# Inverting the delta rule's triangular blocks with 64 stationary columns and vector-engine transposes

## The reference, cut to what matters

```python
    m = jnp.where(strict, jnp.einsum("nbhid,nbhjd->nbhij", kb, kc) * decay, 0.0)
    t = lax.linalg.triangular_solve(eye + m, jnp.broadcast_to(eye, m.shape),
                                    left_side=True, lower=True, unit_diagonal=True)
    u = t @ (vc * bc)
    w = t @ (kb * jnp.exp(cum_g)[..., None])
```

## Time and profile before

| | |
|---|---|
| median of 3 runs | 2893.55 us (2893.49 to 2894.24) |
| span of the profiled execution | 2893.0 us |
| PE busy | 2871.0 us, 99% of the span |
| DVE busy | 1903.8 us, 66% |
| ACT busy | 1399.1 us, 48% |
| DMA engines, mean busy share in the delta rule's stretch (1080 to 1760 us) | 0.41 |

### The profile page before, as it was taken

One profiled execution on the slowest core, in us unless ns is written; L12 is line 12 of the kernel. 1 busy time (PEld: TensorE's weight loads), 2 busy tenths in 40 slices (PEclk: granted clock), 3 DMA queues, 4 the chain that ended last, 5 costly groups with the idle time before them and its releaser, 6 DMA issues.

```text
span 2893.0 us, 39239 instructions
## 1 busy us (share of the span) xinstructions
PE 2871.0 (99%) x16096; PEld 2493.5 (86%) x16096; DVE 1903.8 (66%) x2425; ACT 1399.1 (48%) x1793; POOL 56.8 (2%) x101
## 2 busy tenths in 40 slices
PE   9999999999999999999999999999999999999998
PEld 8899888888888888888888888888888888888887
DVE  7645557678665668787778765456666555565556
ACT  5434644357443445665655653434345434444434
POOL 0000200000000000000000000000000000000000
PEclk9999999999999999999999999999999999999999
DMA  7444445464555544334333355544354454554453
GB/s 279 184 179 161 146 160 200 179 246 170 198 185 179 211 149 156 136 138 140 133 144 130 133 174 190 189 177 161 144 197 182 176 202 182 197 198 180 183 196 145
DMA packets 72850, 506.80 MB, mean 175 GB/s; under 512 B 8384, under 2 KB 8512, under 8 KB 12896
## 3 DMA queue, kind: packets, MB, share of 16 engines
q1 hardware_dynamic: 71136, 497.95, 46.8%
q0 software_dynamic: 1104, 5.90, 0.6%
q10 hardware_dynamic: 432, 0.45, 0.0%
HBM read 500.07 MB, written 2.10 MB: 174 GB/s over the span
## 4 chain that ended last, share of the span: by engine, by line
PE 96%; DVE 2%; ACT 1%; DMA 1%; issue 0%; SPq 0%; POOL 0%; DVEq 0%; ACTq 0%
PE double L1328 87%; PE bank L1328 7%; PE bank L1331 2%; ACT whi L1709 0%; DMA vec<-in_vec 0%; DVE wlo L2064 0%; DMA raw<-in_wall 0%; DVE cacc L2070 0%; DVE acc L2064 0%; ACT L1744 0%; SPq L2854 0%; DMA mblk<-in_memT 0%; ACT AA L1848 0%; DVE rr L2064 0%; ACT L1905 0%
## 5 line engine op out<-in xcount | busy, mean ns | idle before, releaser
L1328 PE MATMUL double<-AA,whi 128*128 128x512 f32 (+1 forms) x5008 | 1656.3, 382 | 3.7 <-DVE wlo L2064 3.6
L1328 PE MATMUL double<-AA,wlo 128*128 128x256 f32 (+1 forms) x4624 | 1300.4, 281 | 0.0
L1709 ACT ACTIVATE whi<-raw 128x1024 fp32r<-128x1024 f32 x926 | 925.0, 1049 | 721.4 <-PE double L1328 689.2
L2064 DVE TENSOR_TENSOR wlo<-raw,whi 128x1024 fp32r<-128x1024 f32 (+1 forms) x934 | 1101.7, 1214 | 236.1 <-ACT whi L1709 234.0
L1328 PEld LDWEIGHTS double<-AA,whi 128*128 128x128 f32 x5008 | 915.4, 188 | 192.5 <-DVE wlo L2064 5.3
L1328 PEld LDWEIGHTS double<-AA,wlo 128*128 128x128 f32 x4624 | 870.9, 188 | 1.5
L1328 PE MATMUL double<-whi,AA 128*128 128x512 f32 x1536 | 489.1, 393 | 0.5 <-DVE wlo L2064 0.5
L1328 PEld LDWEIGHTS double<-whi,AA 128*128 128x128 f32 x1536 | 288.5, 188 | 60.7 <-DVE wlo L2064 1.3
L1328 PE MATMUL double<-whi,BB 128*128 128x512 f32 x1024 | 316.9, 389 | 0.0
L1328 PE MATMUL double<-wlo,AA 128*128 128x512 f32 x768 | 299.1, 390 | 0.0
L1328 PEld LDWEIGHTS double<-whi,BB 128*128 128x128 f32 x1024 | 192.2, 188 | 40.3
(11 more groups left out here) (336 smaller groups left out, 1851.7 us busy)
## 6 DMA issues: line engine op xcount, KB each, us to landing
raw<-in_wall SPq DMA_DIRECT2D x462, 1024.0 KB, 4.8
raw<-in_wall SPq DMA_DIRECT2D x9, 256.0 KB, 7.0
X<-in_xT SPq DMA_DIRECT2D x1, 2048.0 KB, 11.2
Mm<-in_memT POOLq DMA_DIRECT2D x1, 2048.0 KB, 15.5
tmp<-rqk POOLq DMA_DIRECT2D x16, 128.0 KB, 2.2
mblk<-in_memT SPq DMA_DIRECT2D x8, 256.0 KB, 4.5
dec<-in_dec POOLq DMA_DIRECT2D x1, 1536.0 KB, 8.7
hs<-in_hsT SPq DMA_DIRECT2D x4, 272.0 KB, 5.8
```

The source lines that it names most:

```text
L1328: return q.matmul(out, lhsT, rhs, start=start, stop=stop, skip_group_check=True)
L1709: q.activation(whi[j % SPL][:, c], raw[j % RAW][:, c], ACT.Copy).then_inc(S("w_hi"), 1)
L2064: return q.tensor_tensor(out, a, b, o)
```

## The change

The inverse keeps its two products for each width and k, but other operands stand and move in them.

- `Mc` holds both chunks of a k under the same 64 columns (partitions 0 to 63 the early chunk, 64 to 127 the late one), with the identity's negative included: `Mc` = strict part − identity. It lies in the first half of `Mn`. It is the stationary operand of `g_up`, 64 columns in place of 128.
- What moves in `g_up` are the columns of the odd blocks of width d of `TT`, 32 for each half, 64 in all. Since the identity is in the product, the mask also lets the old value through, and `g_down` gives the sum itself: the addition to `Tc` and the tile `Tc` are gone.
- DVE masks the result into `Cm`: 32 columns for each half, on the half's own partitions, the rest of the 64 columns zero from one `memset` of POOL in `begin_gdn`.
- `g_down` multiplies `Td` (the transposed blocks, both chunks under 64 columns, in the first half of `Tn`) with `Cm`. ACT copies the result from PSUM straight into the odd blocks' columns of `TT`, 32 columns a half, in two operations.
- The transposes of PE are gone. DVE transposes the diagonal quarters of `TT` into `Td` by blocks of 32 by 32, two operations a width (for d = 32 one, of the block between), in `g_down`, where it waits for ACT.
- `g_inv0` has no matmul: DVE masks `Mc` to width 1 and transposes it into `TT`.

```diff
@@ make_plan, g_gdn
-        b1, f1 = side.take()
-        r = add("g_inv0", h, b1=b1, f1=f1, p1=up("gdn_pe"), c=up("gdn_vec", 2), x=up("gdn_vec"), xd=up("gdn_act", 2))
+        r = add("g_inv0", h, m=r["m"], n=up("gdn_vec"), x=up("gdn_vec", 2))
...
-            r = add("g_down", (h, d), n=n, c=c, p3=p3, b2=b2, f2=f2, p2=up("gdn_pe"), x=up("gdn_vec"), xd=up("gdn_act", 2))
+            r = add("g_down", (h, d), c=c, b2=b2, f2=f2, p2=up("gdn_pe"), xd=up("gdn_act", 2), n=up("gdn_vec", 2 if d < 32 else 1))
@@ program
+    Mc = [x[:, 0:2, :].rearrange("p a (b c) -> p (a b) c", c=64) for x in Mn]
+    Td = Tn[:, 0:2, :].rearrange("p a (b c) -> p (a b) c", c=64)
@@ tensor_program
         def s_g_up(key, r):
...
             for k in range(4):
-                ins = mm_group(bank[r["b1"]][:, k * 64:(k + 1) * 64], Mn[s][:, k, :], Tc[:, k, :])
-            ins.then_inc(S("gdn_pe"), 1)
-            free(r["f3"])
-            q.wait_ge(S("gdn_act"), r["xd"])
-            for k in range(4):
-                ins = transpose(bank[r["b3"]][:, k * 128:(k + 1) * 128], TT_[s][:, k, :])
+                ins = mm_group(by_block(bank[r["b1"]][EARLY, k * 64:(k + 1) * 64], d), Mc[h % 2][:, k, :], odd(TT_[h % 2][:, k, :], d))
             ins.then_inc(S("gdn_pe"), 1)
 
         def s_g_down(key, r):
             free(r["f2"])
-            q.wait_ge(S("gdn_act"), r["n"])
             q.wait_ge(S("gdn_vec"), r["c"])
             for k in range(4):
-                ins = mm_group(bank[r["b2"]][:, k * 64:(k + 1) * 64], Tn[:, k, :], Cm[:, k, :])
+                ins = mm_group(bank[r["b2"]][EARLY, k * 64:(k + 1) * 64], Td[:, k, :], Cm[:, k, :])
             ins.then_inc(S("gdn_pe"), 1)
@@ scalar_program
         def s_g_down(key, r):
-            q.wait_ge(S("gdn_vec"), r["x"])
-            onto_diagonal(key[0] % 2)
+            h, d = key
+            q.wait_ge(S("gdn_pe"), r["p2"])
+            for n, x in enumerate(HALF):
+                for_x = bh(r["b2"])[EARLY, :, n * 32:(n + 1) * 32].rearrange("p k (b e) -> p k b e", e=d)
+                q.activation(odds(TT_[h % 2][x, :, x], d), for_x, ACT.Copy).then_inc(S("gdn_act"), 1)
@@ vector_program
-            tt(Mn[s][:, :, :], Mf[s][:, :, :], bc("strict"), ALU.mult).then_inc(S("gdn_vec"), 1)
+            for x in HALF:
+                tt(Mc[s][x, :, :], Mf[s][x, :, x], bc("strict")[x, :, :], ALU.mult).then_inc(S("gdn_vec"), 1)
+            q.wait_ge(S("gdn_vec"), r["n"])
+            tt(Mc[s], Mc[s], bc("eye"), ALU.subtract).then_inc(S("gdn_vec"), 1)
...
+            tt(Td, Mc[s], bc("below"), ALU.mult).then_inc(S("gdn_vec"), 1)
+            q.wait_ge(S("gdn_vec"), r["n"])
             for x in HALF:
-                tt(Cm[x, :, :], bk(r["b1"])[x, :, x], bc("m1")[x, :, :], ALU.mult).then_inc(S("gdn_vec"), 1)
-            q.wait_ge(S("gdn_vec"), r["c"])
-            tt(Tc[:, :, :], Cm[:, :, :], bc("eye"), ALU.add).then_inc(S("gdn_vec"), 1)
+                transposed(TT_[s][x, :, x], Td[x, :, :])
...
-            tt(Cm[:, :, :], bh(r["b1"]), bc(f"m{d}"), ALU.mult).then_inc(S("gdn_vec"), 1)
+            for n, x in enumerate(HALF):
+                c = slice(n * 32, (n + 1) * 32)
+                tt(Cm[x, :, c], bh(r["b1"])[EARLY, :, c], bc(f"m{d}")[EARLY, :, :], ALU.mult).then_inc(S("gdn_vec"), 1)
...
         def s_g_down(key, r):
-            q.wait_ge(S("gdn_pe"), r["p2"])
-            tt(Tc[:, :, :], Tc[:, :, :], bh(r["b2"]), ALU.add).then_inc(S("gdn_vec"), 1)
+            h, d = key
+            q.wait_ge(S("gdn_act"), r["xd"])
+            if d < 32:
+                for x in HALF:
+                    transposed(Td[x, :, :], TT_[h % 2][x, :, x])
+            else:
+                transposed(Td[32:64, :, 0:32], TT_[h % 2][0:32, :, 32:64])
```

More of the change, by code:

```diff
@@ L123, in constants @@
     }
-    for d in (1, 2, 4, 8, 16, 32):
-        r, g = p % 64, f[:, 0:64]
-        tab[f"m{d}"] = -1.0 * ((r // (2 * d) == g // (2 * d)) & (g % (2 * d) >= d) & (r % (2 * d) < d))
+    for d in (2, 4, 8, 16, 32):
+        o = w // d * 2 * d + d + w % d
+        tab[f"m{d}"] = -1.0 * (((r // (2 * d) == o // (2 * d)) & (r % (2 * d) < d)) | (r == o))
     for name, v in tab.items():
@@ L819, in g_gdn @@
             b1, f1 = side.take()
[L820 to L823, removed]
+            r = add("g_up", (h, d), x=x, b1=b1, f1=f1, p1=up("gdn_pe"), c=up("gdn_vec", 2), v=up("gdn_vec") if d == 4 else 0)
             side.free(b1, "gdn_vec", r["c"])
-            n, c, p3 = r["n"], r["c"], r["p3"]
+            c = r["c"]
             if d == 2:
@@ L840, in g_gdn @@
         b1, f1 = side.take()
-        b3, f3 = side.take()
-        r = add("g_up64", h, x=x, xd=xd, b1=b1, f1=f1, b3=b3, f3=f3, p1=up("gdn_pe"), p3=up("gdn_pe"), n=up("gdn_act"), c=up("gdn_vec"))
-        side.free(b3, "gdn_act", r["n"])
+        r = add("g_up64", h, x=x, b1=b1, f1=f1, p1=up("gdn_pe"), c=up("gdn_vec"))
         side.free(b1, "gdn_vec", r["c"])
-        n, c = r["n"], r["c"]
+        c = r["c"]
         yield
         b2, f2 = side.take()
-        r = add("g_down64", h, n=n, c=c, b2=b2, f2=f2, p2=up("gdn_pe"), x=up("gdn_vec"))
+        r = add("g_down64", h, c=c, b2=b2, f2=f2, p2=up("gdn_pe"), x=up("gdn_vec"))
         side.free(b2, "gdn_vec", r["x"])
@@ L1283, in bc, with by_block, odd, odds @@
         return C(name).unsqueeze(1).broadcast_to([P_, 4, CON[name][1]])
+    def by_block(x, d):
+        return x.rearrange("p (b e) -> p b e", e=d)
+    def odd(x, d):
+        return x.rearrange("p (b two e) -> p b two e", two=2, e=d)[:, :, 1, :]
+    def odds(x, d):
+        return x.rearrange("p k (b two e) -> p k b two e", two=2, e=d)[:, :, :, 1, :]
     def col(x, h):
@@ L1555, in s_g_up @@
         def s_g_up(key, r):
-            s = key[0] % 2
-            if key[0] >= 2 and key[1] == 2:
-                q.wait_ge(S("cleared"), at["g_clear", key[0] - 2]["z"])
+            h, d = key
             free(r["f1"])
-            q.wait_ge(S("gdn_vec"), r["x"])
+            q.wait_ge(S(r["x"][0]), r["x"][1])
             for k in range(4):
-                ins = mm_group(bank[r["b1"]][:, k * 64:(k + 1) * 64], Mn[s][:, k, :], Tc[:, k, :])
-            ins.then_inc(S("gdn_pe"), 1)
-            free(r["f3"])
-            q.wait_ge(S("gdn_act"), r["xd"])
-            for k in range(4):
-                ins = transpose(bank[r["b3"]][:, k * 128:(k + 1) * 128], TT_[s][:, k, :])
+                ins = mm_group(by_block(bank[r["b1"]][EARLY, k * 64:(k + 1) * 64], d), Mc[h % 2][:, k, :], odd(TT_[h % 2][:, k, :], d))
             ins.then_inc(S("gdn_pe"), 1)
@@ L1588, in s_g_up64 @@
             free(r["f1"])
-            q.wait_ge(S("gdn_vec"), r["x"])
+            q.wait_ge(S(r["x"][0]), r["x"][1])
             for k in range(4):
[L1591 to L1596, removed]
+                ins = mm_group(bank[r["b1"]][EARLY, k * 64:(k + 1) * 64], Mf[s][LATE, k, EARLY], TT_[s][LATE, k, LATE])
             ins.then_inc(S("gdn_pe"), 1)
@@ L1609, in s_g_v @@
             free(r["bf"])
-            q.wait_ge(S("gdn_act"), r["xd"])
+            q.wait_ge(S("gdn_act"), at["g_down", (h, 32)]["xd"])
             q.wait_ge(S("gdn_vec"), at["g_o", (h, 0)]["y"] if t_ else at["g_down64", h]["x"])
@@ L1683, in tensor_program @@
                "mixf": s_mixf, "gab1": s_gab1, "gab2": s_gab2, "rsc": s_rsc, "rav": s_rav, "rtr": s_rtr,
-               "cvn": s_cvn, "g_dec": s_g_dec, "g_mat": s_g_mat, "g_inv0": s_g_inv0, "g_up": s_g_up, "g_down": s_g_down,
+               "cvn": s_cvn, "g_dec": s_g_dec, "g_mat": s_g_mat, "g_up": s_g_up, "g_down": s_g_down,
                "g_x": s_g_x, "g_up64": s_g_up64, "g_down64": s_g_down64, "g_vb": s_g_vb, "g_v": s_g_v, "g_o": s_g_o, "g_tr": s_g_tr, "rmem": s_rmem, "x_s": s_x_s,
@@ L2048, in scalar_program @@
                "gta_sig": token_sigmoid(None), "rtr": s_rtr, "rav": s_rav, "begin_gdn": s_begin_gdn, "cvs": s_cvs, "cvq": s_cvq, "cvn": s_cvn,
-               "gz_sig": token_sigmoid(lambda h, m: gz[m][:, :]), "gtb_sig": token_sigmoid(None), "g_dec": s_g_dec, "g_inv0": s_g_inv0, "g_up": s_g_up, "g_down": s_g_down,
-               "g_up64": s_g_up64, "g_nrm": s_g_nrm, "memn": s_memn, "mv": s_mv, "a4": s_a4, "x_s": s_x_s,
+               "gz_sig": token_sigmoid(lambda h, m: gz[m][:, :]), "gtb_sig": token_sigmoid(None), "g_dec": s_g_dec, "g_down": s_g_down,
+               "g_nrm": s_g_nrm, "memn": s_memn, "mv": s_mv, "a4": s_a4, "x_s": s_x_s,
                "a6": s_a6, "f1": s_f1}
@@ L2493, in s_begin_gdn @@
             q.wait_ge(S("ret_m"), RET_END)
[L2494 removed]
+            q.wait_ge(S("zeroed"), 4)
         last_cv = [0]
@@ L2839, in gpsimd_program @@
                 q.memset(cst[:, :, 0:3], 0.0).then_inc(S("zeroed"), 1)
-                for z in TT_:
+                for z in (Cm, *TT_):
                     q.memset(z[:, :, :], 0.0).then_inc(S("zeroed"), 1)
```

58 lines of the change are left out of this document (20 added, 38 removed).

## The result

| | before | after |
|---|---|---|
| median of 14 runs each | 2893.52 us (2891.24 to 2894.83) | 2887.26 us (2886.26 to 2889.33) |
| ratio, 95% interval | | 0.9979 (0.9972 to 0.9987) |
| span of the profiled execution | 2893.0 us | 2886.2 us |

What follows compares the result with a forecast made beforehand. PE was taken as the bound, 96% of the chain. Savings of 22.4 (transposes) and 7.2 (products) less 2.0 of waits gave 27.6 us, so 2865.9 us from 2893.55; range 2853 to 2875 us.

Steps and rivals of the forecast that it cites:

- PE's transposes: In `g_up`, `g_up64` and `g_inv0`: all PE transposes go, about 0.39 to 0.45 us a group, 22.4 us saved.
- The products: In `g_up` and `g_down`: 64 columns for 128 save 0.09 us in each of 80 groups, 7.2 us.
- DVE's prices: DVE in the delta rule: 0.42 us a transpose, 0.28 a mask; 22 us more work, fitting into 151 idle.
- the first rival: PE's products pay no edge on a mode change, 0.65 us a group; 38.6 us less, 2854.9 us; chance 0.15.
- the one with transposes of 0.69: DVE's transposes take 0.69 us, so PE waits 0.25 us in each of 40 widths; 2875.9 us; chance 0.10.
- the one in which waits eat the whole gain: PE's transposes are replaced by an equal amount of waiting in the delta rule, so nothing changes; chance 0.02.
- the signs of being wrong: PE idle 10 us or more ahead of the inverse's products, products above 0.89 us, or loss outside the delta rule.
- the waits: PE waits for DVE only in the last pair of heads: 0.90 us for one mask, 2.0 in all.
- ACT's delay: In `g_down`: ACT's two half-size copies come no later than DVE's former operation by more than some 0.3 us.
- room: DVE's next mask had 1.33 us to spare in the tight place, 0.29 left; DVE idle 151 of 680 us.
- The rival of the other side: DVE's wait for ACT's copies becomes the bound; 1.0 us in each of 40 widths gives 2904 us; chance 0.05.
- if time is lost in a stretch without the delta rule: One of the signs that would show the forecast wrong; no size was given.

Runs made afterwards that it cites:

- e6: The kernel before with each group of PE's transposes of `TT` issued twice; 2913.13 us, ratio 1.0069, 20.2 us more for 48 groups.
- e2: The changed kernel without DVE's transposes in `g_down` and without their wait for ACT, inverse not computed; 2871.54 us, ratio 0.9922.
- e3: The changed kernel with DVE's transposes reading the ready `Mc` into an unread tile, no wait for ACT, inverse not computed; 2873.99 us, ratio 0.9931.
- e1: The changed kernel with 224 unused columns behind its constants, so later tiles lie where the kernel before had them; 2882.95 us, ratio 0.9960.
- e9: The kernel before with 32 unused columns (128 bytes) behind its constants; 2899.96 us, ratio 1.0023.
- e10: The changed kernel with DVE's transposes moved to the head of `g_up` and 96 unused columns behind the constants; 2875.06 us, ratio 0.9936.

## Why the prediction was wrong

**The parts that held.** PE's transposes: 22.4 us forecast for 56 groups, 18.8 of it for the 48 that e6 doubles, which cost 20.2. The products: 1.15 us a group with the edge of 0.21, as forecast; both terms together 29.6 forecast, 30.2 in e2. DVE's prices: 0.44 and 0.28 us against 0.42 and 0.28. Taking the moving columns in runs of d costs nothing to be seen: `bank<-TT,Mn` and `bank<-Cm,Tn` both have 227 ns. The 0.05 us that the first rival puts at the way back rests on no row, and no run separates it. The rival without an edge is refuted by the timeline, the one with transposes of 0.69 by their row, and the one in which waits eat the whole gain by e2. Of the signs of being wrong, idle time ahead of `bank<-TT,Mn` and `bank<-Cm,Tn` is 6.7 us and not 10: the sign looked at the wrong groups.

**The step that failed: the waits, forecast 2.0 us.** The transposes and what waits behind them cost 15.7 us (median of after less median of e2; spans: 16.7). The last pair of heads, where the forecast put all of its 2.0, is not where it failed: PE's waits there went from 2.1 to 3.5 us, 1.4 more, though it was the mask that cost more (1.9 in place of 0.90) and the wait ahead of `g_up` that shrank to 1.6. The rest of the stretch was put at nothing. The forecast spoke of the chain: "The weaker place is DVE: it works in order, stands until ACT has copied". It then priced that standing at nothing there, with two arguments that do not hold. The first was ACT's delay, "no later by more than some 0.3 us", taken from the length of the copies. What counts is what stands ahead of them on ACT: `cacc_r` and two splits, 2.4 us from 1310.52 to 1312.96. The trace of the kernel before had the same three operations ahead of the same copies. The second was room. The forecast looked only at the next mask, in one place with 1.33 us to spare, and at DVE's idle time as an average over the stretch, 151 of 680 us. Where the copies came late, the next 27 us of DVE's queue had 1.6 us of idle time, and the waits appeared at `t` and `U`. The forecast named "the convolution's work", to which `t` belongs, as standing in that queue, but priced only the mask; `U`, in the same queue, it never named.

The rival of the other side was this very mechanism. Its bound, 0.74 us of waiting in each of the 40 widths, was not reached: 16.7 / 40 = 0.42, so the kernel stayed faster. But it was given 0.05 and one price for all widths or none. It does not come in every width. DVE stood 23 times, and PE paid for it chiefly after d = 16, where `cacc_r` and two splits stand ahead of the copies on ACT and a full queue behind the transposes on DVE.

**A term that was missing: the layout, 5.0 us.** The diff shortens the constants by 224 columns, which moves the tiles behind. The forecast named "if time is lost in a stretch without the delta rule" as a sign against it, and that is what happened. No row of the kernel before could price it.

**The account, by spans.** Before 2893.0; PE's terms −29.6, 2863.4; layout +5.0, 2868.4; e2 shows 2869.5, so 1.1 us are left over; the transposes and their wait +16.7, 2886.2. By the medians of e2 and e3 some 2.5 us of the last term are load and 13.3 standing (by spans 5.2 and 11.5; the profile of e3 is of its slowest run); the split is no sharper than that.

**What stays open.** How much of the standing is ACT's lateness, as said at e3. The delta rule's weight products themselves, those without side work between, run slightly longer with the change: matmuls of `AA` with `whi` take 244.4 ns from start to start against 242.4, some 2 us in all, and 245.8 with the old layout. And it isn't shown why a shift of the tiles slows the products with `BB` while it makes the later ones with `AA` moving, a tile that was not shifted, faster (237.2 to 235.6 ns; with the `wlo` products this gives some 4 of 8.2 us back).

## What to carry to other kernels

When a step gets a wait for another in-order engine, price it by what stands ahead of its releaser on that engine and by the idle time in the next stretch of its own queue, row by row; an average of idle time says nothing about either. Moving such a step to where its result is needed gave back 5.8 us here, but only part of the loss, since what stands behind it there waits in turn. And when a change resizes a tile, ask what it moves behind it; pad it first, so that only the change itself is measured.

## What was not expected of the hardware

- The place of tiles within a partition of the on-chip memory changes the rate of PE's products. For 1024 products with `BB` standing and 512 columns of `whi` moving, a shift of `BB` and all tiles behind the constants by +128 or −896 bytes lengthens the median from 389 to 393 ns, and one of −512 does not (after, e1, e9, e10). Over the whole kernel that is 5 us. The same form with the unshifted `AA` standing stays at 389 ns. That it is `BB`'s own place and not that of another shifted tile is thus likely, but no run moved `BB` alone.
- DVE's transpose of 64 by 256 fp32 by 32 by 32 blocks takes 439 ns, little more than a copy of as many elements a partition (0.42 us). The Trainium skill's 311 ns ("VectorE: DVE Perf Modes", The three transpose paths) is for 128 by 128 in bf16, a form that no run here has.
- A group of 128 by 64 products costs 0.80 us where 128 by 128 cost 0.89: with half the stationary columns PE gains only 0.09. The first of them comes 0.21 us behind the last weight product in place of 0.11, which takes 0.10 of what could be gained.
